# Three attention stages rewritten: dilated attention by query classes over 688 keys, values as split products over 512 queries

## The chip, the cores and the metric

One Trainium2 chip, one core of it. The number is the device time of one execution of the whole program in microseconds (us). A profiled execution gives, beside its own time, the span from its first to its last instruction and every instruction in it.

## What is computed

Two blocks over 1024 tokens of width 1024, everything in float32. The first block runs a differential attention and a neighbourhood attention (8 heads, each query sees 640 keys at most, with a bias table), an output product and a gate. The second block has two layers; each runs a dilated attention (8 heads of 64), a latent attention (8 heads, 96 wide in the scores, 64 in the values), an output product and an MLP. What the change touches are three of these attentions:

```python
DIL_CONFIGS = ((128, 1), (512, 4), (2048, 16))
def dilated_attention(q, k, v, pos, slopes):
    for window, dil in DIL_CONFIGS:      # query t attends to t + j*dil, |j*dil| <= window/2
        o, lse = dilated_branch(q, k, v, pos, slopes, window, dil)   # scores - slope[h]*|pos_q - pos_k|
    wts = jax.nn.softmax(jnp.stack(lses), axis=0)
    return jnp.sum(jnp.stack(outs) * wts[..., None], axis=0)
def latent_attention(...):
    s = (einsum(qn, k_nope) + einsum(qr, k_rot)) * scale
    p = softmax(s)                       # all 1024 keys
    return einsum(p, v)
```

The three branches of the dilated attention are one softmax in which a key counts once for every branch that holds it. Beyond a distance of 256 only keys at a multiple of 16 count, and from 64 to 256 only those at a multiple of 4.

## The kernel before

The program is written engine by engine, by hand: each engine (TensorE for products, ScalarE, VectorE, GpSimd, and SyncE, which issues most DMAs) runs its own list in the order in which it is written, and semaphores with counted values tie the lists together. Stages follow one another, with a barrier of all engines between them.

An attention stage has 64 units: 8 heads times 8 tiles of 128 queries. `softmax_pv_pe` gives TensorE's order: `scores(u+1)`, `turn(u)`, `pv(u-1)`. `scores` multiplies one 128-query tile by the keys into a pair of PSUM banks (512 columns each); keys and, in the latent stage, queries are held as two fp32r parts, a rounded high one and the rest, so that float32 precision comes out of two or three fp32r products. The maximum over the keys (`maxes`, VectorE) and the exponential (`exps`, ScalarE) follow. `turn` transposes the 128x128 tiles of the probabilities through TensorE; `copy_turned` brings them from PSUM to SBUF, half on ScalarE (L906), half on VectorE (L908). `pv` multiplies them by the values in plain float32, one product of 128 columns for each key tile (L881); the rows of this line count two instructions for each such product. `output` divides by the sum of the exponentials.

In the neighbourhood stage GpSimd makes the bias of each unit: once for each head it adds the column mask to a table `NAB` that SyncE has loaded (L1392, L1376), then for each unit it adds a row mask (L1395). In the dilated stage ScalarE scales a table of distances for each unit (L1427), GpSimd adds the logarithm of how often a key counts (L1400), over all 1024 keys.

After the latent stage `nt` transposes the attention's output for the output product: ScalarE writes the high part `XTh` (L492), VectorE the low one `XTl` (L529), both from PSUM.

## Time and profile before

| | |
|---|---|
| median of 3 executions | 4692.28 us (4685.75 to 4693.0) |
| the profiled execution | 4690.71 us, of which its span is 4688.9 us |
| neighbourhood attention | from 768 to 994 us in the span |
| dilated attention, two layers | from 1547 to 1815 and from 3274 to 3541 us |
| latent attention, two layers | from 1815 to about 2095 and from 3541 to about 3824 us |
| TensorE busy | 87% of the span |
| mean granted TensorE clock | 0.948 of 2.4 GHz |

The rows below are read so: a row of the timeline is start, duration, engine, line of the kernel, operation, output and inputs by the program's names, count; in brackets stands the idle time before it and what ended it. A matmul's duration is its latency; what it costs in a run of like ones is the distance from one start to the next. `PE` is TensorE, `DVE` VectorE, `ACT` ScalarE, `POOL` GpSimd, `SPq` SyncE's queue.

### The profile page before, as it was taken

The numbers are of one execution on the slowest core, as the hardware profiler recorded it, in microseconds if no ns is written. First come the engines' busy times: TensorE is split into PE (matmuls) and PEld (weight loads), VectorE is DVE, ScalarE is ACT, GpSimd is POOL, SyncE is SP. The second block draws the span as 40 slices with busy tenths as digits, with TensorE's granted clock in tenths as the row PEclk, the third lists the DMA queues.
The fourth block names the chain that finished last, engine by engine and source line by source line (L and its number), as shares of the span: only waits on it lengthen the run. The fifth ranks groups of instructions, "written<-read, shape, count | busy, mean of one in ns | idle before, by whom it ended". The sixth has DMA issues, their size and how long they took to land.

```text
span 4688.9 us, 60744 instructions
## 1 busy us (share of the span) xinstructions
PE 4082.2 (87%) x22152; PEld 3480.2 (74%) x22152; DVE 2228.0 (48%) x4269; ACT 1503.3 (32%) x2417; POOL 1736.7 (37%) x1140
## 2 busy tenths in 40 slices
PE   3999575788789798998899999688898996999998
PEld 2788465776577687886688888576887885888887
DVE  2443585532366565553444443465565544323323
ACT  2221243431233674441221211232773432222221
POOL 2432123531255462002544444353560003544442
PEclk9999888999899899998999999899999998999999
DMA  6765332631135422212223221245322221111111
GB/s 152 207 179 149 98 89 64 138 100 50 72 88 140 111 60 66 48 50 90 78 84 108 77 99 32 76 119 146 84 55 63 54 80 49 50 49 54 45 45 50
DMA packets 300704, 404.65 MB, mean 86 GB/s; under 512 B 45908, under 2 KB 224980, under 8 KB 299860
## 3 DMA queue, kind: packets, MB, share of 16 engines
q1 hardware_dynamic: 293496, 375.60, 28.5%
q10 hardware_dynamic: 6912, 25.17, 1.8%
q8 instruction: 178, 2.92, 0.3%
q14 instruction: 118, 0.97, 0.1%
HBM read 316.23 MB, written 93.63 MB: 87 GB/s over the span
## 4 chain that ended last, share of the span: by engine, by line
PE 68%; issue 8%; DVE 7%; POOL 5%; DMA 3%; SPq 2%; DVEq 2%; ACT 2%; POOLq 1%; ACTq 0%
PE ps L881 10%; PE ps L456 6%; PE ps L458 5%; PE ps L457 5%; PE ps L871 5%; PE ps L1834 5%; PE ps L1835 5%; PE ps L1836 5%; PE ps L1850 5%; PE ps L1852 4%; PE ps L1851 4%; POOL rs L770 2%; PE ps L917 1%; DVEq L1235 1%; PE ps L1507 1%
## 5 line engine op out<-in xcount | busy, mean ns | idle before, releaser
L405 POOL TENSOR_TENSOR WL<-RAW,WH 128x1024 fp32r<-128x1024 f32 x226 | 556.6, 2476 | 1195.1 <-ACT WH L387 1184.9
L456 PE MATMUL ps<-WH,XTh 128*128 128x512 f32 (+1 forms) x1536 | 616.9, 402 | 70.6 <-issue 34.8
L457 PE MATMUL ps<-WH,XTl 128*128 128x512 f32 (+1 forms) x1536 | 604.2, 393 | 0.0
L458 PE MATMUL ps<-WL,XTh 128*128 128x512 f32 (+1 forms) x1536 | 604.0, 393 | 0.0
L387 ACT ACTIVATE WH<-RAW 128x1024 fp32r<-128x1024 f32 x226 | 234.1, 1057 | 794.2 <-PE ps L1852 347.8
L1870 DVE TENSOR_TENSOR X<-ps,X 128x512 f32<-128x512 f32 x512 | 349.0, 689 | 254.1 <-PE ps L1852 253.1
L1850 PE MATMUL ps<-WH,Hh 128*128 128x512 f32 x1024 | 401.3, 392 | 4.3 <-DVE X L1870 4.0
L1834 PE MATMUL ps<-XTh,WH 128*128 128x512 f32 x1024 | 400.4, 391 | 1.2 <-issue 1.2
L1835 PE MATMUL ps<-XTl,WH 128*128 128x512 f32 x1024 | 398.9, 390 | 0.0
L1836 PE MATMUL ps<-XTh,WL 128*128 128x512 f32 x1024 | 398.8, 389 | 0.0
L1852 PE MATMUL ps<-WL,Hh 128*128 128x512 f32 x1024 | 398.6, 389 | 0.0
L1851 PE MATMUL ps<-WH,Hl 128*128 128x512 f32 x1024 | 398.5, 389 | 0.0
L456 PEld LDWEIGHTS ps<-WH,XTh 128*128 128x128 f32 x1536 | 296.5, 193 | 133.4 <-issue 72.0
L1400 POOL TENSOR_TENSOR BI<-BI,TB 128x1024 f32<-128x1024 f32 x128 | 303.5, 2373 | 225.7 <-ACT BI L1427 223.8
L1861 DVE TENSOR_TENSOR MT<-ps,MT 128x512 f32<-128x512 f32 x128 | 88.5, 692 | 609.1 <-ACT MT L1878 609.1
L458 PEld LDWEIGHTS ps<-WL,XTh 128*128 128x128 f32 x1536 | 295.3, 192 | 58.8
L457 PEld LDWEIGHTS ps<-WH,XTl 128*128 128x128 f32 x1536 | 296.6, 193 | 54.2
L1890 POOL TENSOR_TENSOR Hl<-MT,Hh 128x512 fp32r<-128x512 f32 x128 | 165.7, 1295 | 460.0 <-ACT Hh L1882 460.0
L881 PE MATMUL ps<-VS,PTr 128*128 128x128 f32 x2688 | 335.1, 277 | 0.0
L881 PEld LDWEIGHTS ps<-VS,PTr 128*128 128x128 f32 x2688 | 319.6, 194 | 0.0
L917 PE MATMUL ps<-KHs,QS 128*128 128x512 f32 (+1 forms) x512 | 218.4, 428 | 102.5 <-DMA slp<-slopes 40.8
L1411 DVE CUSTOM_DVE_ANT_0 Sb<-ps,BI 128x1024 f32<-128x1024 f32 (+1 forms) x192 | 209.5, 1091 | 171.6 <-PE ps L918 86.1
(196 smaller groups left out, 7664.0 us busy)
## 6 DMA issues: line engine op xcount, KB each, us to landing
RAW<-w_all SPq DMA_DIRECT2D x232, 512.0 KB, 4.0
WM<-w_mod ACTq DMA_DIRECT2D x48, 512.0 KB, 4.2
WM<-w_mod SPq DMA_DIRECT2D x48, 512.0 KB, 4.0
QS<-QA_d SPq DMA_DIRECT2D x24, 512.0 KB, 3.9
KHs<-KA_d SPq DMA_DIRECT2D x48, 256.0 KB, 6.0
KLs<-KA_d SPq DMA_DIRECT2D x48, 256.0 KB, 6.5
VS<-VA_d SPq DMA_DIRECT2D x20, 512.0 KB, 7.3
X<-x SPq DMA_DIRECT2D x2, 4096.0 KB, 12.8
```

The lines of the kernel that those rows point to most:

```text
L405: e.tensor_tensor(w_low(n), w_raw(n), w_high(n).bitcast(F32), ALU.subtract).then_inc(w_ready, 1)
L456: e.matmul(bank, a, w, start=(kc == 0), stop=False)
L457: e.matmul(bank, b, w, start=False, stop=False)
L458: j = e.matmul(bank, a, l, start=False, stop=(kc == K - 1))
L881: i = e.matmul(ps[:, 6 + u % 2, 0:P], ptbuf[:, u % 2, k, :], vbuf[:, h % 2, key, :], start=(k == 0), stop=(k == len(kt) - 1))
L1834: e.matmul(bank, w, xh, start=(kc == 0), stop=False)
L1835: e.matmul(bank, w, xl, start=False, stop=False)
L1836: j = e.matmul(bank, l, xh, start=False, stop=(kc == KC - 1))
L1850: e.matmul(bank, Hh[:, half, et, tq], w, start=(et == 0), stop=False)
L1851: e.matmul(bank, Hl[:, half, et, tq], w, start=False, stop=False)
L1852: j = e.matmul(bank, Hh[:, half, et, tq], l, start=False, stop=(et == 1))
L1870: e.tensor_tensor(X[:, t, cs], ps[:, 4 + (step * 16 + k) % (3 if mod else 4), :], X[:, t, cs], ALU.add).then_inc(s["yt"], 1)
```

## The change

The three stages get new code; the unit (128 queries of a head) and the number of units stay.

**Values in split parts over 512 queries.** In all three stages the transposed probabilities are now split like the keys: ScalarE writes the high part (`high`), VectorE the rest (`low`), into tiles `PTh` and `PTl` that hold a group of four units, 512 queries. The values are held side by side as high and low part, 64 columns each (`VHL`, made once for each head by `value_high` on ScalarE and `value_low` on GpSimd). `values` multiplies them with 512 query columns at a time as two fp32r products for each key tile. The result comes out transposed; `copy_out` brings it to SBUF, and four float32 products with `twoI` (two identity matrices, one above the other) turn it back and add the two halves. In the latent stage these stand in `turn_back` (L1723), in the other two ahead of the scores of every fourth unit (L1395), in columns of a score bank that the scores leave free.

**Dilated attention by classes.** A unit is now 128 queries of one class modulo four (every fourth query of one half of the sequence). Such a class needs 576 keys as they stand, and of the other 448 only those of its own class: 688 keys. Queries, and the far keys, are read with a stride of four elements. The bias is held in `ND` for all eight tiles of a head, scaled so that the next head's follows from it by adding a table to a quarter of the near and to all far columns (`dil_pool`); the queries' norm takes the head's slope up (`by_head`, one more small GpSimd instruction for each of 8 tiles in a layer).

**One more unit in flight.** In the neighbourhood and dilated stages (`band_pe`) there are three buffers of probabilities, scores run two units ahead, and the transposes are split: four tiles ahead of the scores, the rest behind the values.

Since the dilated output stands in class order, the `nt` behind the latent stage writes 4 of its 8 column blocks with a stride of four elements.

```diff
+DIL_FAR = 112
+DIL_KEYS = 576 + DIL_FAR
+N_UNITS, N_GROUPS = 64, 16
...
+                        to, got = XTh[:, kc, g * 512:g * 512 + 512], ps[:, turn_bank(n), :]
+                        if kc < classes:
+                            to, got = by_class(to), got.rearrange("p (r a) -> p r a", r=4)
+                        e.activation(to, got, ACT.Copy).then_inc(s["hi"], 1)
...
+        class Dilated:
...
+            def __init__(self, u):
+                g, c = divmod(u % T, 4)
+                self.g, self.first, self.width = g, 0, DIL_KEYS
...
+                self.queries = slice(512 * g + c, 512 * g + 512, 4)
+                if g == 0:
+                    far = slice(576 + c, S, 4)
...
+                    self.keys = [(slice(0, 512), 0), (slice(512, 576), 512), (far, 576)]
...
+        def band_pe(who, a):
...
+            def scores(u):
...
+                if u >= 2:
+                    e.wait_ge(s["max"], a.u0 + min(u - 1, N_UNITS))
+                if hosts_back(u - 2) is not None:
+                    e.wait_ge(s["out"], a.g0 + hosts_back(u - 2) + 1)
+                G = hosts_back(u)
+                if G is not None:
+                    e.wait_ge(s["ot_copied"], a.g0 + G + 1)
+                    for r in range(4):
+                        c = at.back + 64 * r
+                        j = e.matmul(flat(2 * (u % 2), c, c + 64), a.OT[:, G % 2, r * P:r * P + P], twoI[:], start=True, stop=True)
+                    j.then_inc(s["back"], 1)
...
+                for keys, c in at.keys:
+                    to = flat(2 * (u % 2), c, c + len(range(S)[keys]))
+                    e.matmul(to, Q[:, h % 2, at.queries], KH[:, h % 2, keys], start=True, stop=False)
+                    j = e.matmul(to, Q[:, h % 2, at.queries], KL[:, h % 2, keys], start=False, stop=True)
+                j.then_inc(s["full"], 1)
...
+            def turn_first(u):
+                at = band(a, u)
+                e.wait_ge(s["exp"], a.u0 + u + 1)
+                ge(e, s["lo"], 2 * (a.u0 + u) - 3)
+                for k in range(4):
+                    c = at.nat + k * P
+                    j = e.transpose(ps[:, 4 + u % 2, k * P:k * P + P], Pt[:, u % 3, c:c + P], ident[:])
+                j.then_inc(s["tr"], 1)
+            def turn_rest(u):
+                at = band(a, u)
+                ge(e, s["lo"], 2 * (a.u0 + u))
+                for src, c in at.rest:
+                    j = e.transpose(ps[0:src.stop - src.start, 7, c:c + P], Pt[:, u % 3, src], ident[:])
+                j.then_inc(s["tr"], 1)
...
+            def values(G, part):
...
+                    rows, key = (slice(0, 64), 4) if g == 0 else (slice(64, P), 3)
+                    v = a.VHL[rows, slot, key, :]
+                    e.matmul(ps[:, 6, :], v, a.PTh[rows, o, 4, :], start=False, stop=False)
+                    e.matmul(ps[:, 6, :], v, a.PTl[rows, o, 4, :], start=False, stop=False)
+                    for r in range(4):
+                        v, c = VFHL[:, slot, 4 * g + r, :], slice(r * P, r * P + P)
+                        e.matmul(ps[:, 6, c], v, a.PTh[0:DIL_FAR, o, 5, c], start=False, stop=False)
+                        j = e.matmul(ps[:, 6, c], v, a.PTl[0:DIL_FAR, o, 5, c], start=False, stop=(r == 3))
...
+            scores(0)
+            scores(1)
+            for u in range(N_UNITS + 6):
+                G, r = divmod(u - 1, 4)
+                if u < N_UNITS:
+                    turn_first(u)
+                scores(u + 2)
+                if 1 <= G <= N_GROUPS and r < 3:
+                    values(G - 1, r)
+                if u < N_UNITS:
+                    turn_rest(u)
...
+        def band_act(who, a):
...
+            def value_high(h):
+                e.wait_ge(*a.v_loaded(h // 2))
+                ge(e, s["ot"], a.g0 + 2 * h - 2)
+                o0 = 64 * (h % 2)
+                if a.kind == "dil":
+                    e.activation(VFHL[:, h % 2, :, 0:64], VFS[:, h // 2 % 2, :, o0:o0 + 64], ACT.Copy)
+                e.activation(a.VHL[:, h % 2, :, 0:64], a.VS[:, h // 2 % 2, :, o0:o0 + 64], ACT.Copy)
+                e.drain().then_inc(s["vhi"], 1)
+            value_high(0)
...
+            for u in range(N_UNITS + 6):
+                if 1 <= u <= N_UNITS:
+                    high(u - 1)
+                if u + 1 < N_UNITS:
+                    exps(u + 1)
+                if u % 4 == 0 and u >= 8:
+                    copy_out(u // 4 - 2)
+                if u % T == 5 and u + 3 < N_UNITS:
+                    value_high(u // T + 1)
...
+        def value_low(e, a, h):
...
+            e.tensor_tensor(a.VHL[:, h % 2, :, 64:128], a.VS[:, h // 2 % 2, :, o0:o0 + 64],
+                            a.VHL[:, h % 2, :, 0:64].bitcast(F32), ALU.subtract)
+            e.drain().then_inc(s["vlo"], 1)
...
+        def na_pool(who, a):
+            e, s = who.e, a.s
+            value_low(e, a, 0)
+            for u in range(N_UNITS):
+                h, t = divmod(u, T)
+                if t == 0:
+                    e.wait_ge(*a.loaded(h))
+                    nab = NAB[:, h % 2, :].rearrange("p (a b) -> p a b", b=GRID_W)
+                    e.tensor_tensor(nab, nab, rows3(CMK[:], NA_E, GRID_W), ALU.add)
+                    e.drain()
+                if u >= 3:
+                    e.wait_ge(s["max"], a.u0 + u - 2)
+                e0 = (NA_START[t] - 2 * t + 8) * GRID_W
+                e.tensor_tensor(BIn[:, u % 3, :], NAB[:, h % 2, e0:e0 + NA_KEYS], RMK[:, NA_KIND[t], :], ALU.add).then_inc(s["bias"], 1)
+                if u % T == 7 and u + 1 < N_UNITS:
+                    value_low(e, a, u // T + 1)
+        def dil_pool(who, a):
...
+                e.wait_ge(s["max"], a.u0 + u + 1)
+                if g == 0:
+                    parts = [(slice(c, 576, 4), slice(128, 272)), (slice(576, DIL_KEYS), slice(272, 384))]
+                else:
+                    parts = [(slice(0, DIL_FAR), slice(0, 112)), (slice(DIL_FAR + c, DIL_KEYS, 4), slice(112, 256))]
+                for cols, table in parts:
+                    j = e.tensor_tensor(ND[:, t, cols], ND[:, t, cols], LM[:, table], ALU.add)
+                j.then_inc(s["bias"], 1)
+                if t == 7:
+                    value_low(e, a, h + 1)
...
+        def heads_pe(who, a):
...
+            def values(G, part):
...
+                for n in range(3 * part, min(3 * part + 3, T)):
+                    v = a.VHL[:, h % 2, n, :]
+                    e.matmul(ps[:, 6, :], v, a.PTh[:, G % 2, n, :], start=(n == 0), stop=False)
+                    j = e.matmul(ps[:, 6, :], v, a.PTl[:, G % 2, n, :], start=False, stop=(n == T - 1))
+                if part == 2:
+                    j.then_inc(s["ot"], 1)
+            def turn_back(G):
+                e.wait_ge(s["ot_copied"], a.g0 + G + 1)
+                ge(e, s["out"], a.g0 + G)
+                for r in range(4):
+                    j = e.matmul(ps[:, 7, 64 * r:64 * r + 64], a.OT[:, G % 2, r * P:r * P + P], twoI[:], start=True, stop=True)
+                j.then_inc(s["back"], 1)
...
+            scores(0)
+            for u in range(N_UNITS + 4):
+                G, r = divmod(u, 4)
+                if u + 1 < N_UNITS:
+                    scores(u + 1)
+                if u < N_UNITS:
+                    turn(u)
+                if G >= 1 and r < 3:
+                    values(G - 1, r)
+                if G >= 1 and r == 3:
+                    turn_back(G - 1)
...
+        def heads_act(who, a):
...
+            def high(u):
+                G, r = divmod(u, 4)
+                if r == 0:
+                    ge(e, s["ot"], a.g0 + G - 1)
+                for b in range(2):
+                    e.wait_ge(s["tr"], 2 * (a.u0 + u) + 1 + b)
+                    e.activation(a.PTh[:, G % 2, 4 * b:4 * b + 4, r * P:r * P + P],
+                                 ps[:, 4 + b, :].rearrange("p (k q) -> p k q", q=P), ACT.Copy).then_inc(s["hi"], 1)
...
+        def heads_dve(who, a):
...
+            def low(u):
+                G, r = divmod(u, 4)
+                for b in range(2):
+                    e.wait_ge(s["hi"], 2 * (a.u0 + u) + 1 + b)
+                    at = (slice(None), G % 2, slice(4 * b, 4 * b + 4), slice(r * P, r * P + P))
+                    e.tensor_tensor(a.PTl[at], ps[:, 4 + b, :].rearrange("p (k q) -> p k q", q=P),
+                                    a.PTh[at].bitcast(F32), ALU.subtract).then_inc(s["lo"], 1)
```

TensorE's order in the latent stage before (`KMh`, `KMl` keys, `QMh`, `QMl` queries, `Pm` probabilities, `PTm` the same transposed, `VSm` values), one unit:

```order
L881 MATMUL ps<-VSm,PTm 128x128 x8
L1507 MATMUL ps<-KMh,QMh 128x512
L1508 MATMUL ps<-KMl,QMh 128x512
L1509 MATMUL ps<-KMh,QMl 128x512
L1507 MATMUL ps<-KMh,QMh 128x512
L1508 MATMUL ps<-KMl,QMh 128x512
L1509 MATMUL ps<-KMh,QMl 128x512
L871 MATMUL ps<-ident,Pm 128x128 x8
```

And now, from the last scores of a unit to the first of the next but one, at the fourth unit of one group and the first of the next:

```order
L1695 MATMUL ps<-KMh,QMl 128x512
L1703 MATMUL ps<-ident,Pm 128x128 x8
L1723 MATMUL ps<-twoI,OTm 128x64 x4
L1693 MATMUL ps<-KMh,QMh 128x512
...
L1703 MATMUL ps<-ident,Pm 128x128 x8
L1714 MATMUL ps<-PThm,VHLm 128x512
L1715 MATMUL ps<-PTlm,VHLm 128x512
L1714 MATMUL ps<-PThm,VHLm 128x512
L1715 MATMUL ps<-PTlm,VHLm 128x512
L1714 MATMUL ps<-PThm,VHLm 128x512
L1715 MATMUL ps<-PTlm,VHLm 128x512
```

The eight 128-column products behind every unit's transposes are gone; behind those of three units of four stand six, six and four 512-column ones, and behind the fourth the four that turn back.

TensorE's order in the dilated stage before (`QS` queries, `KHs`, `KLs` keys, `Pb` probabilities), one unit:

```order
L871 MATMUL ps<-ident,Pb 128x128 x8
L881 MATMUL ps<-VS,PTr 128x128 x8
L917 MATMUL ps<-KHs,QS 128x512
L918 MATMUL ps<-KLs,QS 128x512
L917 MATMUL ps<-KHs,QS 128x512
L918 MATMUL ps<-KLs,QS 128x512
```

And now (`Pd` probabilities, `VFHL` the values of the far keys), the iteration with the last third of a group's values:

```order
L1411 MATMUL ps<-ident,Pd 128x128 x4
L1401 MATMUL ps<-KHd,QSd 128x112
L1402 MATMUL ps<-KLd,QSd 128x112
L1401 MATMUL ps<-KHd,QSd 128x64
L1402 MATMUL ps<-KLd,QSd 128x64
L1401 MATMUL ps<-KHd,QSd 128x512
L1402 MATMUL ps<-KLd,QSd 128x512
L1441 MATMUL ps<-PThd,VHLd 128x512
L1442 MATMUL ps<-PTld,VHLd 128x512
L1445 MATMUL ps<-PThd,VFHL 128x128
L1446 MATMUL ps<-PTld,VFHL 128x128
...
L1418 MATMUL ps<-ident,Pd 112x128 x2
```

Two of the four 512-column score products are replaced by four narrow ones, and the transposes are six; L1445 and L1446 stand there four times each.

GpSimd's order in the neighbourhood stage before, at the change of a head, with what the instructions wait for (`heads_max` is VectorE's maximum, `na_ld` SyncE's loads of the head):

```order
L1395 TENSOR_TENSOR BI<-NAB,RMK 128x640 [waits heads_max] x7
L1392 TENSOR_TENSOR NAB<-NAB,CMK 128x1152 [waits heads_max,na_ld1]
L1395 TENSOR_TENSOR BI<-NAB,RMK 128x640
```

And now (`heads_vhi` is ScalarE's `value_high`, which stands behind the exponential of the head's seventh unit):

```order
L1597 TENSOR_TENSOR BIn<-NAB,RMK 128x640 [waits heads_max] x5
L1580 TENSOR_TENSOR VHLn<-VSn,VHLn 128x8x64 [waits heads_vhi]
L1592 TENSOR_TENSOR NAB<-NAB,CMK 128x1152 [waits na_ld1]
L1597 TENSOR_TENSOR BIn<-NAB,RMK 128x640 [waits heads_max] x8
```

The split of the next head's values has come between the last bias of a head and the table of the next, with a wait for ScalarE in front of it.

## Rows read from the trace of the kernel before

**Rows 1.** Windows by stage: us, busy time of each engine, granted clock, DMA share, GB/s

```profile
core 0: us, PE busy (x) PEld busy (x) DVE busy (x) ACT busy (x) POOL busy (x), PEclk, DMA share, GB/s
1547.00:1815.00 268.00, 240.44 (x1792) 214.52 (x1792) 159.65 (x387) 185.49 (x264) 151.75 (x64) 0.95 0.29 70
1815.00:2124.00 309.00, 286.89 (x2040) 260.60 (x2041) 167.53 (x336) 120.86 (x212) 9.39 (x4) 0.97 0.24 57
3274.00:3541.00 267.00, 240.49 (x1792) 214.79 (x1792) 159.63 (x387) 185.62 (x264) 151.77 (x64) 0.95 0.28 70
...
793.40:996.80 203.40, 160.84 (x1208) 150.21 (x1208) 108.06 (x384) 90.47 (x192) 115.13 (x70) 0.94 0.49 103
1566.00:1813.50 247.50, 236.84 (x1785) 212.04 (x1784) 158.67 (x384) 174.89 (x254) 150.64 (x64) 0.98 0.23 55
1825.40:2095.30 269.90, 264.42 (x1920) 241.59 (x1920) 158.06 (x320) 108.46 (x192) 0.00 (x0) 0.99 0.21 48
```

**Rows 2.** Timeline of TensorE, one unit of the latent stage

```profile
2019.38 0.48 PE L1507 MATMUL ps<-KMh,QMh 96*128 96x512 f32 x1
2019.70 0.40 PE L1508 MATMUL ps<-KMl,QMh 96*128 96x512 f32 x1
2019.94 0.39 PE L1509 MATMUL ps<-KMh,QMl 96*128 96x512 f32 x1
...
2020.85 1.04 PE L871 MATMUL ps<-ident,Pm 128*128 128x128 f32 x8
2021.73 1.95 PE L881 MATMUL ps<-VSm,PTm 128*128 128x128 f32 x16
2023.43 0.48 PE L1507 MATMUL ps<-KMh,QMh 96*128 96x512 f32 x1
```

**Rows 3.** Timeline of TensorE, one unit of the dilated stage

```profile
1607.10 1.06 PE L871 MATMUL ps<-ident,Pb 128*128 128x128 f32 x8
1608.00 1.95 PE L881 MATMUL ps<-VS,PTr 128*128 128x128 f32 x16
1609.70 0.48 PE L917 MATMUL ps<-KHs,QS 128*128 128x512 f32 x1
...
1610.72 1.04 PE L871 MATMUL ps<-ident,Pb 128*128 128x128 f32 x8
```

**Rows 4.** Timeline of TensorE: 320-column products in the neighbourhood stage

```profile
802.52 0.30 PE L918 MATMUL ps<-KLs,QS 128*128 128x320 f32 x1
802.67 0.31 PE L917 MATMUL ps<-KHs,QS 128*128 128x320 f32 x1
```

**Rows 5.** Timeline of TensorE: plain float32 products of one column

```profile
196.78 1.84 PE L1686 MATMUL ps<-ones,MA 128*128 128x1 f32 x16
198.49 0.48 PE L456 MATMUL ps<-WH,XTh 128*128 128x512 f32 x1
```

**Rows 6.** Groups by line and shape, latent stage

```profile
L1518 DVE TENSOR_REDUCE mx<-ps 128x1 f32<-128x1024 f32 x64 | 78.3, 1224 | 70.5 <-PE ps L1509 70.5
L1528 ACT ACTIVATE Pm<-ps,nmx 128x1024 f32<-128x1024 f32 x64 | 71.3, 1114 | 170.7 <-DVE nmx L1520 170.7
```

**Rows 7.** Timeline behind the latent stage: 512-column splits from PSUM

```profile
2096.13 4.03 ACT L492 ACTIVATE XTh<-ps 128x512 fp32r<-128x512 f32 x8 [4.51 <-PE ps L558]
2096.84 4.87 DVE L529 TENSOR_TENSOR XTl<-ps,XTh 128x512 fp32r<-128x512 f32 x8 [1.72 <-ACT XTh L492]
```

**Rows 8.** Groups by line and shape, neighbourhood stage

```profile
L1395 POOL TENSOR_TENSOR BI<-NAB,RMK 128x640 f32<-128x640 f32 x64 | 98.3, 1549 | 48.3 <-DVE nmx L1416 46.9
L1436 ACT ACTIVATE Pb<-Sb,nmx 128x640 f32<-128x640 f32 x64 | 53.1, 830 | 136.9 <-DVE nmx L1416 136.9
L1411 DVE CUSTOM_DVE_ANT_0 Sb<-ps,BI 128x640 f32<-128x640 f32 x64 | 52.8, 824 | 65.0 <-POOL BI L1395 53.1 <-PE ps L918 10.7 <-issue 0.4
L1392 POOL TENSOR_TENSOR NAB<-NAB,CMK 128x1152 f32<-128x1152 f32 x8 | 21.1, 2643 | 53.6 <-DMA NAB<-NAB_d 51.9 <-DVE nmx L1416 1.7
```

**Rows 9.** Groups by line and shape, whole span: smaller instructions of the new loops' kinds

```profile
L1890 POOL TENSOR_TENSOR Hl<-MT,Hh 128x512 fp32r<-128x512 f32 x128 | 165.7, 1295 | 460.0 <-ACT Hh L1882 460.0
L710 DVE TENSOR_TENSOR QN<-ps,rs 128x256 f32<-128x256 f32 x80 | 33.6, 420 | 66.9 <-POOL rs L770 65.5 <-PE ps L615 0.9 <-issue 0.4
L908 DVE COPY PTr<-ps 128x128 f32<-128x128 f32 x64 | 18.6, 291 | 8.5 <-PE ps L871 7.3 <-issue 0.3
L768 POOL TENSOR_TENSOR ss<-ss,epsr 128x8 f32<-128x8 f32 x32 | 6.4, 201 | 2.5 <-DVE ss L692 2.5
```

More of the change, by code:

```diff
@@ L110, in shape_tables, with times @@
     onehot[t5_bucket(rel), np.arange(2 * S - 1)] = 1.0
-    j = np.arange(TOEP)[None, :] - (T - 1) * P - np.arange(P)[:, None]
-    many = sum(((np.abs(j) <= w // 2) & (j % d == 0)).astype(np.int32) for w, d in DIL_CONFIGS)
-    logmult = np.where(many > 0, np.log(np.maximum(many, 1)), NEG).astype(np.float32)
+    def times(rel):
+        return sum(((np.abs(rel) <= w // 2) & (rel % d == 0)).astype(np.int32) for w, d in DIL_CONFIGS)
+    query = 4 * np.arange(P)[:, None]
+    many = times(np.arange(1536)[None] - 512 - query)
+    logmult = np.where(many > 0, 2 * np.log(np.maximum(many, 1)), -1e33).astype(np.float32)
+    many = times(4 * np.arange(-128, 256)[None] - query)
+    logstep = (2 * np.log(np.maximum(many, 1))).astype(np.float32)
     c = np.arange(GRID_W)
@@ L814, in in_cell, with qk_kind @@
             return lambda kc: (first + kc // kper, (kc % kper) * width)
-        def qk_kind(dst, gain, first):
+        def qk_kind(dst, gain, first, by_head=False):
             def store(e, t, m, slot):
@@ new lines, in build_program @@
+        class Narrow:
+            def __init__(self, u):
+                self.g = u % T // 4
+                t = u % T
+                self.first = na_tiles(t)[0] - 2 * self.g
+                self.flat, self.width, self.nat, self.back = 0, NA_KEYS, 0, 768
+                self.keys = [(slice(NA_START[t] * GRID_W, NA_START[t] * GRID_W + 512), 0),
+                             (slice(NA_START[t] * GRID_W + 512, NA_START[t] * GRID_W + NA_KEYS), 512)]
+                self.queries = tok(t)
+                self.rest = [(slice(512, NA_KEYS), 0)]
+                self.rest_rows = P
@@ L1976, in layout @@
     out["pos_cols"] = v["positions_2"][0].reshape(T, P).T
+    out["pos_class"] = v["positions_2"][0].reshape(2, P, 4).transpose(1, 0, 2).reshape(P, T)
     out["w_mod"] = v["w_mod_2"]
```

639 lines of the change are left out of this document (381 added, 258 removed).

## The prediction

> **What bounds the kernel now.** I read the windows by stage first, to see how much of the span the three rewritten stages hold: 203 us of the neighbourhood attention from its first maximum on, 268 and 267 us for the dilated in its two layers, and 270 us from the first scores of the latent stage to its last output [rows 1]. In the dilated and latent stretches TensorE is busy for 96% and 98% at a granted clock of 0.98 and more, VectorE and ScalarE for 71% or less. So these two are bound by TensorE, and its own timeline tells what a unit costs. The reader is to look at the distances of starts. Latent: scores to transposes 1.47 us (six 512-column fp32r products at 0.23, and about 0.1 for the change of kind), eight transposes 0.88, sixteen value instructions 1.70, that is 0.106 each; 4.05 in all [rows 2]. Dilated: 3.62, with scores of 1.02 [rows 3]. The neighbourhood stage is another matter: TensorE is busy for 161 of 203 us [rows 1], and GpSimd waits 52 us for the table of a head to land, while VectorE waits 53 us for GpSimd's bias [rows 8].
>
> **Prices on TensorE.** A 512-column fp32r product costs 0.227, a 320-column one 0.15 [rows 2, 4]: in proportion to columns. A plain float32 product is two instructions, and 16 of them take 1.71 us with one column as with 128, 0.107 each [rows 2, 5]; a transpose takes 0.11. I read 0.107 as the least that any product with a 128-column weight costs. Narrower fp32r products than 320 columns (64, 112, 128) are nowhere in the trace, nor operands with a stride of four elements. Lower bound 0.107 each, the floor; upper bound 0.213, the plain float32 product of two instructions [rows 2, 5]. I take 0.14, nearer to the 320-column row, which shows one pass for each column.
>
> The Trainium skill (SBUF — State Buffer, Door 1: The DMA port swizzle) states that SBUF has 16-byte lines and that an access which crosses to a new line each time pays, so float32 strides are free only inside one line. No row here has such a stride. The sum would be 0.107 by the floor and twice that for the strided loads by the rule; this speaks against the classes. Rival A has the same direction, with its price from rows.
>
> **Latent stage.** Removed: 1.70 of values in each unit. Added for four units: sixteen 512-column products, 3.63, with three changes of kind at 0.1, so 0.98 a unit; and four plain products, eight instructions at 0.107 with one change, 0.24 a unit. Unit: 1.47 + 0.88 + 0.98 + 0.24 = 3.57 against 4.05.
> Do the others keep up? ScalarE: exponential 1.11, two splits of 0.50 (8 in 4.03), a quarter of a copy 0.13: 2.3 [rows 6, 7]. VectorE: 1.22 for the maximum, which now negates itself, two low parts at 0.61, a quarter of an output 0.2: 2.65 [rows 6, 7]. The loop that could bind is transposes, two splits, next exponential, next transposes: the first half of the transposes with its latency 0.65, then 0.5 + 0.5 + 1.11 + 0.19 and hand-overs, about 3.0, under 3.57. So it is TensorE still. The stage holds 64 units: 270 - 64 x 4.05 = 11 of filling and emptying. The emptying grows, since three parts of values, a copy, the turning back and one output follow the last split: +3. New stretch 64 x 3.57 + 14 = 242, saves 28; two layers, **-56**. Bounds: 3.5 (smaller changes of kind) and 3.8 (the loop through ScalarE at a third longer), -65 and -27.
>
> **Dilated stage.** Scores: 0.454 for the two wide products, four narrow at 0.14, change 0.1: 1.11. Transposes: six at 0.11, 0.66. Values for four units: ten 512-column products 2.27, eight of 128 at 0.14 = 1.12, three changes: 0.92 a unit. Turning back 0.24. Sum 2.93; with all narrow ones at the floor 2.73, at 0.213 3.37. VectorE: maximum over 688, by the 640-column row 0.87 and the read behind it 0.1; low parts 0.61 and, for 256 columns, 0.42; output 0.2: 2.2 [rows 7 to 9]. ScalarE: 0.9 + 0.5 + 0.3 + 0.13 + 0.15 = 2.0 (the scaling of the distances is gone). GpSimd: the 640- and 1152-column rows give 0.2 + 0.00214 a column [rows 8], so two adds of 144 and 112 columns 0.95, and two value splits a head, 2 x 1.3 / 8 [rows 9]: 1.3, with eight units of slack. The third buffer lets scores run ahead, so that TensorE need not wait for a chain of 1.6 (split, exponential) inside 2.9.
> Start: the eight distance tiles, value splits and first biases come one after another; I put the second maximum where the first stood before, no gain. The stretch was 247.5 [rows 1], 64 x 3.62 = 232 and 15 around it; I leave 12, since the drains of TensorE at the end of each head go and the emptying is longer. 64 x 2.93 + 12 = 199.5, saves 48; two layers, **-96**. Bounds -122 and -40.
>
> **Neighbourhood stage.** TensorE: scores 0.454 + 2 x 0.14 + 0.1, five transposes 0.55, twelve value products a group (2.72 + 0.3) / 4, turning back 0.24: 2.4; VectorE 0.82 + 0.1 + 0.61 + 0.29 + 0.3 = 2.1 [rows 7 to 9]. The 52 us of waiting for the table should go: it is now asked for when the scores of the head before last are through, ahead of the values and gates, which come only once in two heads. Something is late next: at the change of a head GpSimd must wait for `value_high`, which stands behind the seventh exponential. From that unit's maximum: exponential 0.83, high part 0.5, low part 1.3, table 2.64, bias 1.55, hand-overs 0.5, 7.3 in all [rows 8, 9], where two units of 2.4 were to pass: 2.5 late, seven heads, 17. The first bias also waits for the values' load, now behind the table's, and their split: some 2.5 + 0.5 + 1.3, +4.5. New: 64 x 2.4 + 17 + 8 for emptying = 179 from the first maximum, against 203 [rows 1]; less 4.5: **-20**. Bounds: -45 (no lateness, 2.3 a unit), 0.
>
> **The rest.** The strided `nt` (8 of 16 evictions in a layer, at most doubled, 0.5 each) and the extra GpSimd instruction for 16 tiles (0.2 [rows 9], with a drain): +5, bounds 0 and +15.
>
> **Sum.** -56 - 96 - 20 + 5 = -167, on the profiled execution's 4690.7 us: 4524. The median of the runs shown lies 1.6 above it; I say **4523**.
>
> **Rivals.**
> *A. Narrow or strided products cost what plain float32 does.* For it: no row shows one cheap. Against: the 320-column row is in proportion to the 512-column one. Dilated units above 3.2, up to 3.37; neighbourhood 2.55. With 3.37: +0.44 x 128 + 0.15 x 64 = +66: 4589. Chance 0.25, from 4560 up. The rule of the Trainium skill cited above would come out here.
> *B. The floor everywhere, and no lateness at the heads.* -0.2 x 128 - 17 - 6, and some 8 in the latent stage: 4466. For it: three buffers may swallow the lateness. Chance 0.23, below 4490.
> *C. Slower: strided weights are read one by one.* All six products of a dilated unit load 128 queries with the stride. At a price p each the unit is 1.9 + 6p (1.9 is 2.93 without its six score products). It ends on the other side when the unit is 167 / 128 = 1.3 above 2.93, at p = 0.39, nearly four times the floor; at 0.5 the unit is 4.9, and the kernel 4523 + 252 = 4775. Nothing in the trace speaks for so much. Chance 0.04.
> *D. The gain goes back in waits.* The loop through ScalarE and VectorE locks both stages to about 4.0 and 3.5: 4690 or so. Against: the sums above leave 0.5 on the tightest. Chance 0.03.
>
> **Chances and range.** The forecast 0.45 (4490 to 4560), A 0.25, B 0.23, C 0.04, D 0.03. A difference of 0.2%, 9 us, is about what a measurement of this kernel can tell from none. Faster: the first three, 0.93; same 0.02 (part of D); slower 0.05 (C and a part of D). The range takes in most of A and B: 4445 to 4600.
>
> **What would show it.** Latent unit 3.57 between the starts of scores, TensorE without gaps, 16 value products at 0.227. In the dilated stage the distances of the 64-, 112- and 128-column products decide between forecast, A and C; 0.11 to 0.14 against 0.21 or more. VectorE or ScalarE busy over 90% of a stage would show my engine sums wrong. In the neighbourhood stage no wait for the load of `NAB`, and a wait of GpSimd in front of `VHLn` once a head, with VectorE's maximum late behind it by 2.5. Wrong I am if the narrow products cost more than two plain instructions, if a hand-over in the four-engine loop is longer than those seen, or if loads of strided far rows of the values are late.

## The result and the profile after

The changed kernel takes 4520.4 us (median of 4, 4515.2 to 4525.5) against 4689.0 (4684.7 to 4693.0): a ratio of 0.964, 95% interval 0.9624 to 0.9657. The forecast was 4523. That the total is right to 3 us owes something to chance: two terms of the sum were wrong by about 30 us each, in opposite directions. (The sum itself gives 4525, not 4523: 4690.7 - 167 is 4523.7, and the median stood 1.6 above the profiled execution, not under it.)

The profiled execution of the changed kernel took 4525.45 us, its span is 4523.6, its mean granted clock 0.942. To see the terms I cut both spans at TensorE's first score product of each stage and at the first transpose of the attention's output (`Y`) behind it. Three of these cuts in the changed kernel, and one of the kernel before, in TensorE's timeline:

```profile
1540.64 0.82 PE L1401 MATMUL ps<-KHd,QSd 128*128 128x512 f32 x1 [20.05 <-DMA KLd<-KA_d]
...
1772.15 0.76 PE L1693 MATMUL ps<-KMh,QMh 96*128 96x512 f32 x1 [11.15 <-DMA KMl<-KM_d]
...
2001.07 3.68 PE L580 MATMUL ps<-ident,Y 128*128 128x128 f32 x32 [1.06 <-DVEq L362]
```

```profile
1825.49 0.77 PE L1507 MATMUL ps<-KMh,QMh 96*128 96x512 f32 x1 [12.53 <-DMA VSm<-VM_d]
```

| from cut to cut, us | before | after | difference | forecast |
|---|---|---|---|---|
| neighbourhood | 208.0 | 187.5 | -20.5 | -20 |
| dilated, layer 1 and 2 | 263.1, 264.2 | 231.5, 233.9 | -61.9 | -96 |
| latent, layer 1 and 2 | 270.0, 271.6 | 228.9, 228.1 | -84.6 | -56 |
| all that lies between | 3412.1 | 3413.8 | +1.7 | +5 |
| span | 4688.9 | 4523.6 | -165.3 | -167 |

The windows of the changed kernel answer to [rows 1]: neighbourhood from its first maximum, dilated (layer 1) from its first maximum, latent in both layers. The window of the dilated stage before, 247.5 us, began 1.4 us ahead of its first maximum.

```profile
core 0: us, PE busy (x) PEld busy (x) DVE busy (x) ACT busy (x) POOL busy (x), PEclk, DMA share, GB/s
799.28:976.80 177.52, 148.27 (x889) 124.56 (x890) 133.40 (x304) 114.37 (x279) 123.59 (x77) 0.97 0.46 93
1542.70:1762.20 219.50, 210.85 (x1178) 191.17 (x1178) 131.63 (x288) 128.92 (x290) 91.75 (x148) 0.95 0.27 65
1772.10:2001.10 229.00, 224.19 (x1281) 190.56 (x1282) 163.42 (x224) 151.86 (x280) 10.25 (x8) 0.98 0.20 49
3428.80:3656.90 228.10, 222.30 (x1281) 188.87 (x1281) 163.33 (x224) 151.75 (x280) 10.24 (x8) 0.99 0.20 48
```

TensorE is still busy for 96% and more of the dilated and latent stretches, so it is still what bounds them, and the error must lie in the prices of its instructions. The neighbourhood stretch is 177.5 us long; the forecast said 179.

**A dilated unit**, answering to [rows 3]:

```profile
1644.05 0.38 PE L1418 MATMUL ps<-ident,Pd 128*128 128x128 f32 x2
1644.27 0.60 PE L1411 MATMUL ps<-ident,Pd 128*128 128x128 f32 x4
1644.63 0.60 PE L1401 MATMUL ps<-KHd,QSd 128*128 128x512 f32 x1
1645.06 0.40 PE L1402 MATMUL ps<-KLd,QSd 128*128 128x512 f32 x1
1645.30 0.19 PE L1401 MATMUL ps<-KHd,QSd 128*128 128x64 f32 x1
1645.33 0.40 PE L1402 MATMUL ps<-KLd,QSd 128*128 128x64 f32 x1
1645.56 0.45 PE L1401 MATMUL ps<-KHd,QSd 128*128 128x112 f32 x1
1645.83 0.41 PE L1402 MATMUL ps<-KLd,QSd 128*128 128x112 f32 x1
1646.07 0.44 PE L1436 MATMUL ps<-PThd,VHLd 128*128 128x512 f32 x1
...
1650.11 0.27 PE L1445 MATMUL ps<-PThd,VFHL 112*128 112x128 f32 x1
1650.21 0.28 PE L1446 MATMUL ps<-PTld,VFHL 112*128 112x128 f32 x1
```

Read the distances of starts. The six score products take 1.44 us (1644.63 to 1646.07) where I had 1.11, that is 0.24 each on average, as much as one of 512 columns. (Single distances between products of unequal width say little: here they run from 0.03 to 0.43, and the one of 0.43 is that of the first wide product in either order of the keys.) But the 128-column products of the far values (L1445, L1446), whose weights have no stride, cost 0.11. So the price is not one of narrow products. The weight loads (`PEld`) show where it sits; these are their groups in the dilated and then in the neighbourhood stage:

```profile
L1402 PEld LDWEIGHTS ps<-KLd,QSd 128*128 128x128 f32 x191 | 62.6, 328 | 0.4
L1401 PEld LDWEIGHTS ps<-KHd,QSd 128*128 128x128 f32 x190 | 60.9, 321 | 0.2
```

```profile
L1402 PEld LDWEIGHTS ps<-KLn,QSn 128*128 128x128 f32 x124 | 24.4, 196 | 2.8
L1401 PEld LDWEIGHTS ps<-KHn,QSn 128*128 128x128 f32 x124 | 24.1, 195 | 10.3 <-issue 7.5
```

The same 128x128 queries take 325 ns to load with the stride of four, 196 without, and in front of them the load path stands idle for 0.6 us in the whole stretch: they come back to back. Their own timeline, in the same unit:

```profile
1645.07 0.32 PEld L1401 LDWEIGHTS ps<-KHd,QSd 128*128 128x128 f32 x1
1645.30 0.31 PEld L1402 LDWEIGHTS ps<-KLd,QSd 128*128 128x128 f32 x1
```

One load starts 0.23 us after the other, and that is what each product costs.

**A latent unit**, answering to [rows 2]:

```profile
1885.87 1.04 PE L1703 MATMUL ps<-ident,Pm 128*128 128x128 f32 x8
1886.66 0.48 PE L1714 MATMUL ps<-PThm,VHLm 128*128 128x512 f32 x1
...
1888.14 0.40 PE L1693 MATMUL ps<-KMh,QMh 96*128 96x512 f32 x1
...
1889.53 1.04 PE L1703 MATMUL ps<-ident,Pm 128*128 128x128 f32 x8
```

Transposes 0.79 us, six value products 1.48 with the change of kind, six score products 1.39 without one. I had charged the change of 0.1 to both.

### The profile page after: what moved, and what is told of

It reads as the page before. It is cut to its first block, busy times and chain, and to the rows that moved or that the text cites. A ratio compares the mean times of both kernels' runs of the same rounds, so it can differ in the third digit from the quotient of the medians.

```text
span 4523.6 us, 53378 instructions
## 1 busy us (share of the span) xinstructions
PE 3936.4 (87%) x19336; PEld 3311.0 (73%) x19336; DVE 2218.5 (49%) x3805; ACT 1522.8 (34%) x2761; POOL 1658.0 (37%) x1369
## 4 chain that ended last, share of the span: by engine, by line
PE 68%; issue 8%; DVE 7%; POOL 5%; DVEq 3%; ACT 3%; DMA 2%; POOLq 2%; SPq 2%; ACTq 0%
PE ps L469 6%; PE ps L470 6%; PE ps L471 6%; PE ps L2181 5%; PE ps L2183 5%; PE ps L2182 5%; PE ps L2197 5%; PE ps L2199 5%; PE ps L2198 5%; PE ps L1703 2%; PE ps L1401 2%; PE ps L1402 2%; POOL rs L795 2%; PE ps L1411 1%; DVEq L1219 1%
## 5 line engine op out<-in xcount | busy, mean ns | idle before, releaser
L400 ACT ACTIVATE WH<-RAW 128x1024 fp32r<-128x1024 f32 x226 | 233.8, 1058 | 794.3 <-PE ps L2199 347.2
L2197 PEld LDWEIGHTS ps<-WH,Hh 128*128 128x128 f32 x1024 | 192.1, 188 | 52.9 <-DVE X L2217 13.6
L2225 ACT ACTIVATE MT<-ps 128x512 f32<-128x512 f32 x128 | 76.4, 597 | 452.6 <-PE ps L2183 449.1
L2181 PEld LDWEIGHTS ps<-XTh,WH 128*128 128x128 f32 x1024 | 192.6, 188 | 41.7 <-issue 2.0
L2183 PEld LDWEIGHTS ps<-XTh,WL 128*128 128x128 f32 x1024 | 192.5, 188 | 40.3
L2199 PEld LDWEIGHTS ps<-WL,Hh 128*128 128x128 f32 x1024 | 192.2, 188 | 40.3
```

The source lines that it names most:

```text
L400: e.activation(w_high(n), w_raw(n), ACT.Copy).then_inc(w_rounded, 1)
L2181: e.matmul(bank, w, xh, start=(kc == 0), stop=False)
L2183: j = e.matmul(bank, l, xh, start=False, stop=(kc == KC - 1))
L2197: e.matmul(bank, Hh[:, half, et, tq], w, start=(et == 0), stop=False)
L2199: j = e.matmul(bank, Hh[:, half, et, tq], l, start=False, stop=(et == 1))
```

## The experiments

Each is an edit of the changed kernel, which stands at 4520.4 us. The kernel before stood at 4687 to 4691 beside them. "In the stage" means from cut to cut as above.

**1. Queries as they stand.**

```diff
-                self.queries = slice(512 * g + c, 512 * g + 512, 4)
+                self.queries = tok(u % T)
```

> Left out: the classes on the query side. In the dilated stage the 128 queries of a unit are taken as they stand, without the stride of four; the far keys keep theirs, so the output is not that of the reference. All else as in the changed kernel. In the changed kernel a dilated unit takes 3.23 us on TensorE, of which the six score products with their change of kind hold 1.51. Theory S (the strided weights cost the time): two wide products 0.46, four narrow ones at 0.11 as in the neighbourhood stage, change 0.1, so 1.0; unit 2.72, 128 units: -65 us, about 4455; the weight loads of these products fall from 325 to about 190 ns. Rival M (the stride of the moving far keys, or narrowness itself, costs it): no change, 4520, and the loads may get shorter without effect.

Measured: 4457.3 (4453.6 to 4460.8), -63. The dilated stages take 199.5 and 202.4 us in place of 231.5 and 233.9. Eight groups of four units begin 86.7 us apart (1601.85 to 1688.59), 2.71 a unit. The loads as a group, two of them, and the six products of one unit, of the other half of the sequence; in the changed kernel such a unit's six take 1.59 (1657.30 to 1658.89):

```profile
L1402 PEld LDWEIGHTS ps<-KLd,QSd 128*128 128x128 f32 x186 | 36.5, 196 | 1.4
```

```profile
1643.69 0.19 PEld L1401 LDWEIGHTS ps<-KHd,QSd 128*128 128x128 f32 x1
1643.81 0.19 PEld L1402 LDWEIGHTS ps<-KLd,QSd 128*128 128x128 f32 x1
```

```profile
1643.50 0.34 PE L1401 MATMUL ps<-KHd,QSd 128*128 128x112 f32 x1
1643.65 0.30 PE L1402 MATMUL ps<-KLd,QSd 128*128 128x112 f32 x1
1643.76 0.24 PE L1401 MATMUL ps<-KHd,QSd 128*128 128x64 f32 x1
1643.83 0.28 PE L1402 MATMUL ps<-KLd,QSd 128*128 128x64 f32 x1
1643.95 0.48 PE L1401 MATMUL ps<-KHd,QSd 128*128 128x512 f32 x1
1644.26 0.39 PE L1402 MATMUL ps<-KLd,QSd 128*128 128x512 f32 x1
1644.49 0.38 PE L1418 MATMUL ps<-ident,Pd 128*128 128x128 f32 x2
```

0.99 us for the six, and the loads start 0.12 us apart. Theory S holds to 2 us.

**2. Far keys as they stand.**

```diff
-                    far = slice(576 + c, S, 4)
+                    far = slice(576 + DIL_FAR * c, 576 + DIL_FAR * c + DIL_FAR)
```

> Left out: the classes on the key side. In the dilated stage the 112 far keys of a unit are a contiguous block, the queries keep their stride of four; the output is not that of the reference. Theory S (strided weights): no change, 4520, the 112-column products keep distances of 0.23 to 0.27 us. Rival M (strided moving columns): the two 112-column products fall from about 0.25 to 0.11 each, -0.28 us a unit, 128 units: -36 us, about 4485.

Measured: 4518.4 (4515.9 to 4523.9), no change. A stride of four in the moving columns costs nothing that can be measured here, as long as the weights are what TensorE waits for. Experiment 1 says the same where the weights load quickly: its 112-column products still have the strided keys, and all four narrow ones take 0.45 us together. (The diff shows one half of the sequence; the other is changed alike.)

**3 and 4. Other strides.**

```diff
-                self.queries = slice(512 * g + c, 512 * g + 512, 4)
+                q0 = 512 * g + 256 * (c // 2) + c % 2
+                self.queries = slice(q0, q0 + 256 - c % 2, 2)
```

```diff
-                self.queries = slice(512 * g + c, 512 * g + 512, 4)
+                self.queries = slice(4 * g + c, S, 8)
```

> Changed: in the dilated stage the 128 queries of a unit are taken with a stride of two elements in place of four; the output is not that of the reference. Two of a unit's queries then stand in the same 16 bytes. If what counts is how many of a load's elements share 16 bytes and two are enough (the Trainium skill, SBUF - State Buffer, says so of reads), the loads take the unstrided time and the kernel is that of the run with contiguous queries, about 4455. If every stride costs alike, no change, 4520. If the cost grows with the bytes spanned, in between, about 4490, with loads of some 250 ns.

> Changed: in the dilated stage the 128 queries of a unit are taken with a stride of eight elements in place of four; the output is not that of the reference. If each element costs one access of 16 bytes wherever it stands, no change against the changed kernel: 4520, loads of 325 ns. If the cost grows with the stride, loads well over 400 ns, a unit above 3.8 us, and above 4590 in all.

Measured: stride two 4460.9 (4458.0 to 4469.8), as without a stride; stride eight 4535.1 in its one run. The loads, of stride two and then of eight:

```profile
L1402 PEld LDWEIGHTS ps<-KHd,QSd 128*128 128x128 f32 x183 | 36.5, 199 | 1.1
```

```profile
L1402 PEld LDWEIGHTS ps<-KLd,QSd 128*128 128x128 f32 x184 | 62.0, 337 | 0.2
```

196, 199, 325, 333 ns for strides of one, two, four, eight: a step between two and four, not a slope. The Trainium skill (SBUF — State Buffer, Door 1: The DMA port swizzle) says that two accesses to one 16-byte line are enough for full bandwidth, and float32 elements at a stride of two are just that. These runs agree, and the rule that the prediction set beside rival A came out in direction and, by the distance between loads (0.12 us without the stride, 0.23 with it), in size. Stride eight is 15 us above the changed kernel, of which some 7 stand in the dilated stages (236.9 and 236.0); with one run I make nothing of it.

**5. The value split later (neighbourhood).**

```diff
-                if u % T == 7 and u + 1 < N_UNITS:
-                    value_low(e, a, u // T + 1)
+                if t == 2 and h:
+                    value_low(e, a, h)
```

> Nothing is left out. In the neighbourhood stage GpSimd makes the low part of the next head's values behind the third bias of that head, not between the last bias of a head and the table of the next. In the changed kernel the half of a head with the change takes 12.1 us, the other 9.17, so 2.9 us are lost at each of 7 changes. Theory (GpSimd stands still for ScalarE's high part, 3.6 us, and then is late): the loss goes, 7 x 2.9 = -20, and the first bias comes 1.3 earlier: about 4499. Rival (GpSimd's own work of 16.4 us a head, or VectorE held up by it, sets the pace): at most half of it, 4510 to 4520.

Measured: 4504.8 (4499.0 to 4505.9), -15.6; in the stage 168.1 for 187.5, so -19.4. GpSimd at the change of a head in the changed kernel, and in this run:

```profile
858.08 1.29 POOL L1580 TENSOR_TENSOR VHLn<-VSn,VHLn 128x512 fp32r<-128x512 f32 x1 [3.61 <-ACTq L1499]
859.55 2.65 POOL L1592 TENSOR_TENSOR NAB<-NAB,CMK 128x1152 f32<-128x1152 f32 x1 [0.18 <-issue]
```

```profile
862.65 1.58 POOL L1597 TENSOR_TENSOR BIn<-NAB,RMK 128x640 f32<-128x640 f32 x1 [1.27 <-DVEq L1527]
864.19 2.65 POOL L1592 TENSOR_TENSOR NAB<-NAB,CMK 128x1152 f32<-128x1152 f32 x1
```

The wait of 3.61 us for ScalarE's high part is gone from in front of the table. VectorE's waits for a bias, other than the stage's first of 25 to 26 us, fall from 9.9 us to 0.7. The half of a head with the change goes from 12.1 to 10.05 us, the other from 9.17 to 8.88, so a difference of 1.2 stays between them. The first bias did not come earlier, as I had expected (8.4 us behind the first scores, 8.3 in the changed kernel): the first head's split still stands in front of its table.

**6. Queries copied by class.** The diff is cut: `queries` is `tok(u % T)` as in experiment 1, and TensorE reads `QCd` and waits for `qc`.

```diff
+            def by_classes(h):
+                e.wait_ge(*a.loaded(h))
+                e.activation(QCd[:, h % 2, :].rearrange("p (g r i) -> p g r i", g=2, r=4),
+                             QSd[:, h % 2, :].bitcast(F32).rearrange("p (g i r) -> p g r i", g=2, r=4), ACT.Copy).then_inc(s["qc"], 1)
...
+                if a.kind == "dil" and u % T == 3 and u + 5 < N_UNITS:
+                    by_classes(u // T + 1)
```

> Nothing is left out. In the dilated stage ScalarE copies each head's queries once into the order of the classes (a strided read of 1024 columns, one instruction a head, at the fourth unit of the head before), and TensorE loads them from there without a stride. Theory S: the gain of the run with contiguous queries, 63 us, less what the copy costs: ahead of the first scores some 1.5 us in each layer, and ScalarE goes from 2.35 to about 2.55 us a unit, still under 2.72: about 4462. Rival: ScalarE becomes the bound or the exponential behind the copy is late once a head (2 x 8 x 1.5 = 24): about 4485.

Measured: 4470.1 (4466.7 to 4478.0), -50; in the stages 202.5 and 204.5. That lies between theory (4462) and rival (4485), nearer to the theory. The copy takes longer than I reckoned from a contiguous one of 1024 columns:

```profile
L1506 ACT ACTIVATE QCd<-QSd 128x1024 fp32r<-128x1024 f32 x7 | 14.5, 2067 | 0.0
```

**7. Scores one unit ahead.**

```diff
-            scores(1)
-            for u in range(N_UNITS + 6):
+            for u in range(N_UNITS + 7):
                 G, r = divmod(u - 1, 4)
+                scores(u + 1)
                 if u < N_UNITS:
                     turn_first(u)
-                scores(u + 2)
```

> Nothing is left out. In the neighbourhood and dilated stages the scores run one unit ahead, not two: they stand ahead of the first transposes of the unit before, as in the kernel before. Theory (the dilated stage is TensorE's alone, and one unit of lead covers maximum and exponential, 2.2 us, with 2.9 us of other work of TensorE): nothing in the dilated stage; in the neighbourhood stage 2.3 us stand against 2.2, so 0 to 0.2 a unit: 4520 to 4533. Rival (the third buffer is what lets TensorE run without gaps): 0.3 us a unit in all three stretches, 192 units, +58: 4578.

Measured: 4734.8 (4733.0 to 4741.2), slower by 214 than the changed kernel, and by 43 than the kernel before beside it. Both theories miss. In the stages: neighbourhood 243.1 for 187.5, dilated 306.6 and 310.5. Two of the waits of the dilated stage, from 1620 to 1780 us (engine, line, what it waited for; us in all, times, longest):

```profile
DVE Pd L1524 <- PE ps L1402: 82.8, 36, 4.0
...
PEld ps L1418 <- DVE PTld L1540: 30.6, 27, 1.9
```

The last transposes of a unit wait for the low parts of the unit before; on VectorE these stand behind the next maximum, which waits for scores that TensorE has only just made. I had counted the cover of the exponential, and not this ring.

**8. One ahead, low parts first.** The same, with VectorE's order turned:

```diff
-                if u + 1 < N_UNITS:
-                    maxes(u + 1)
                 if 1 <= u <= N_UNITS:
                     low(u - 1)
+                if u + 1 < N_UNITS:
+                    maxes(u + 1)
```

> Nothing is left out. As the run with the scores one unit ahead, but VectorE makes the low parts of a unit ahead of the maximum of the unit after the next, not behind it. Theory (what cost 214 us there was a ring: the last transposes of a unit wait for the low parts of the unit before, these stand on VectorE behind a maximum, and that waits for scores which TensorE has only just done): the ring is open, the dilated stage back at 3.23 us a unit, the neighbourhood stage at 2.3 to 2.5, 4520 to 4535. Rival (the second unit of lead is needed as such, for maximum and exponential): waits for the exponential take the place of those for the low parts, 4700 or more.

Measured: 4642.8 (4639.3 to 4649.5), +122. The order of VectorE was 92 of the 214 us; the other 122 stay as long as the scores run only one unit ahead. Dilated 257.8 and 260.6, neighbourhood 244.3. The chain in the dilated stage, VectorE and then ScalarE:

```profile
1680.32 0.86 DVE L1524 CUSTOM_DVE_ANT_0 Pd<-ps,ND 128x688 f32<-128x688 f32 x1
...
1682.73 0.69 DVE L1536 TENSOR_TENSOR PTld<-ps,PThd 128x512 fp32r<-128x512 f32 x1 [1.54 <-ACT PThd L1479]
...
1683.67 0.86 DVE L1524 CUSTOM_DVE_ANT_0 Pd<-ps,ND 128x688 f32<-128x688 f32 x1
```

```profile
1681.25 0.87 ACT L1468 ACTIVATE Pd<-Pd,mx 128x688 f32<-128x688 f32 x1 [1.63 <-DVEq L1526]
...
1682.12 0.58 ACT L1479 ACTIVATE PThd<-ps 128x512 fp32r<-128x512 f32 x1
```

Maximum, exponential, high part, low part and the next maximum now follow one after another, 3.35 us from maximum to maximum: two engines take turns. One or two maxima in a group of four come later (3.84 or 4.61 us), so that eight units take 29.05 us (1634.02 to 1663.07), 3.63 each; that is 0.40 over the changed kernel's 3.23, and 64 x 0.40 is the 26 us by which the stage is longer. It is neither of the two theories as I wrote them: the waits are between ScalarE and VectorE, and TensorE waits little for the exponential (2.3 us from 1620 to 1780, where VectorE waits 73 us for ScalarE's high part and ScalarE 72 for the maximum).

**9. Latent values in one block.**

```diff
-                if G >= 1 and r < 3:
-                    values(G - 1, r)
+                if G >= 1 and r == 0:
+                    for part in range(3):
+                        values(G - 1, part)
```

> Nothing is left out. In the latent stage all sixteen value products of a group stand behind the first unit's transposes of the next group, in place of six, six and four behind three units. If a change from a plain float32 or transposing product to an fp32r one costs 0.1 us and a change between values and scores nothing, a group has one such change for each unit in both kernels (five with the turning back), and TensorE's group stays at 13.65 us: 4520, or a little over it where the next exponential is late behind the long block. If each visit of the values costs a change of its own, two visits fewer: 0.2 a group, 32 groups, -6: 4514.

Measured: 4568.9 in one run, +48; the latent stages 248.9 and 247.6 for 228.9 and 228.1. A group takes 14.95 us. Two of its four units now hold only scores and transposes, and there TensorE waits for the exponential:

```profile
1907.28 0.39 PE L1695 MATMUL ps<-KMh,QMl 96*128 96x512 f32 x1
1908.11 1.09 PE L1703 MATMUL ps<-ident,Pm 128*128 128x128 f32 x8 [0.45 <-ACT Pm L1745]
...
1911.04 1.09 PE L1703 MATMUL ps<-ident,Pm 128*128 128x128 f32 x8 [0.45 <-ACT Pm L1745]
```

2.93 us from one to the next: that is the loop through ScalarE, for which the forecast had about 3.0. From the last product's 0.23 us (1907.51) to 1908.11 TensorE does nothing for 0.6 us, twice a group, 1.2 of the 1.3 us that a group is longer; nothing is left for a change of kind that was saved. Both forecasts miss: the late exponential that the first allowed for costs 48 us, not a little.

**10. The turned output as it stands.**

```diff
-                turned = nt(who, TURN, 2 + L, Y, False, out0, classes=4)
+                turned = nt(who, TURN, 2 + L, Y, False, out0)
```

> Changed: the transposed attention output of the second block is written as it stands, not with the stride of four, in all eight column blocks; the columns of the dilated half are then in class order and the output is not the reference's. The first eight evictions took 5.80 us on ScalarE and 6.41 on VectorE in the changed kernel against 4.03 and 4.87, and the first product came 0.6 us later behind the first transposes. Theory (TensorE waits for the last eviction only at the start of the product): 0.6 to 1.5 us a layer, -1 to -3: 4518. Rival (every strided eviction counts, 16 a layer on two engines by 0.25 to 0.4): -8 to -10: 4511.

Measured: 4522.1 (4514.3 to 4528.0), no change. The evictions are as short as before again (611 ns on ScalarE, 743 with the stride) and the time doesn't follow, so the rival's 8 to 10 us aren't there; the theory's 1 to 3 us can't be told from none.

**11. Both repairs.** The edits of 5 and 6; the first head's copy stands behind the second distance tile.

> Nothing is left out. Two repairs together: the queries of the dilated stage copied by class on ScalarE (the first head's copy now stands behind the second distance tile, and has its own load to wait for), and GpSimd's split of the next values behind the third bias in the neighbourhood stage. Their single runs gave -50 and -16 us; the first scores of a dilated stage waited some 5 us longer in the former, because the copy stood behind all sixteen distance instructions, and most of that, 2 x 4, should come back: 4520 - 50 - 16 - 8 = 4446. If the two share a cause they would give less, 4455 to 4470; they stand in different stages with a barrier between, so I expect the sum.

Measured: 4454.9 (4449.1 to 4457.3), 0.9496 of the kernel before (0.9482 to 0.951). It is 65.5 us under the changed kernel, the sum of the single gains (15.6 and 50.3) and no more: moving the first copy brought nothing. The first scores do come some 3 us earlier than in experiment 6 (563.4 and 1194.8 us after the transposes of `Y`, 566.2 and 1198.4 there; the changed kernel has 563.9 and 1193.9). But in the first layer the stage itself lasts 207.9 us in place of 202.5; in the second it is 204.9 and 204.5. The trace shows most of it for the first layer: the first exponential stands 6.6 us behind the first scores (2.9 in experiment 6), since twelve distance instructions and a wait of 2.47 us for the load of the far values are ahead of it on ScalarE. Counted from the transposes of `Y` it comes at 570.0 us, against 569.1: what was moved was not the last thing to be waited for. No run tests this.

## Why the prediction was right, and where not

**What bounds it.** Right: TensorE bounds the dilated and latent stages before and after, at the distances of starts. In the changed kernel VectorE is busy for 60% to 72% of these stretches, ScalarE for 59% to 67%.

**Latent, -56 against -84.6; outside the bounds I gave.** The mechanism was right, the size was not. A group of four units takes 13.65 us, 3.41 a unit, where the sum had 3.57. By its parts, of a group: turning back 0.81 us a group (forecast 0.96), scores 5.63 (5.88), transposes 3.24 (3.52), values 3.97 (3.93). The step at fault is "1.47 + 0.88": both were read where each unit had a change of kind in front of its scores and plain products behind its transposes. Now three of four scores follow the values, which are of their kind (1.39 each), and three of four transposes are followed by fp32r products (0.79). Filling and emptying is 228.9 - 64 x 3.41 = 10.6 us, not 14: the +3 for a longer emptying was wrong too, and is 7 of the 28.6 us by which the forecast missed. Experiment 9 shows that the number of visits to the values is not what counts.

**Dilated, -96 against -61.9.** The step "four narrow at 0.14" failed, in both halves. Narrow products as such cost the floor, 0.11 (L1445 here, and the four narrow scores in experiment 1 on average). With weights at a stride of four, every product costs about 0.235 however few its columns are, for a load starts only every 0.23 us: 6 x 0.235 and the change of 0.1 are the 1.51 us that the scores take in a unit, +0.40 on my sum; transposes are less by 0.05, and values and turning back by 0.04 each: 3.23 measured (12.77 and 13.05 us for alternate groups of four; the parts are those of the shorter), 2.93 forecast. By the prediction's own sign, a dilated unit above 3.2, rival A came out in this stage, and the total of 4520 hides it: the latent stage gave back 28.6 of the 34 us. It is rival A's mechanism for the stride only; at 3.37 it charged the narrow value products too. Rival C named the cause most closely, a price for each strided weight load, but set it at 0.39 and more where 0.235 was measured. Experiments 1 to 4 settle it: unstrided weights give 2.71 a unit (the prediction's sum with all narrow products at the floor was 2.73) and take back 63 us, unstrided moving columns nothing. The emptying, 219.5 - 64 x 3.23 = 12.8, was right.

**Neighbourhood, -20 against -20.5.** The mechanism was right; that the size is right to 0.5 us is partly luck, since the parts err both ways. The halves of a head without a change take 9.17 us (2.29 a unit, forecast 2.4), those with one 12.1, so 2.9 late at a change, forecast 2.5. The emptying is 177.5 - 64 x 2.29 - 7 x 2.9 = 10.6 us, forecast 8. The first maximum is 5.9 us later in the span than before (799.28, 793.39), forecast 4.5. GpSimd does wait for ScalarE ahead of `VHLn`, and the waits of 52 us for the table are gone [rows 8]. Experiment 5 takes VectorE's wait for the late bias away; the stage is 19.4 us shorter.

**The rest, +5 against +1.7.** The strided evictions of `nt` are longer (743 ns on ScalarE over all, 615 before) and cost nothing that experiment 10 could measure.

**The third buffer and the second unit of lead.** I gave them a sentence, and no term: "TensorE need not wait for a chain of 1.6 inside 2.9". The sign was right; experiments 7 and 8 show how much hangs on it. With the other engines' orders as they are, one unit of lead costs 214 us, more than the whole change gains; with VectorE's turned, still 122. In the neighbourhood stage some of that goes with the clock: granted 0.86 in experiment 8, with TensorE busy for 179 of 236 us, against 0.97 and 148 of 177.5 in the changed kernel, for the same products.

## What to carry to other kernels

Price a product by its weight load as well as its columns: a narrow one is cheap only if its weights load quickly, and float32 weights at a stride of four elements do not; one strided copy of them on an engine with room pays at once. Where engines pass a unit round, write down for each wait what stands ahead of it on the engine waited for; the lead in units is a property of all the orders together, and can be worth more than the arithmetic saved.

## What the runs showed of the hardware

- Weight loads of 128x128 fp32r: 196 ns contiguous, 199 at stride two, 325 at four, 333 at eight. In a run of such loads a product costs about 0.11 us at least with the first two and 0.24 with the others. ScalarE pays for the stride as well: 2.07 us for the copy of 1024 columns at a stride of four, where a contiguous split of that width (L400) takes 1.06 on average; whether the stride itself or the pattern of eight blocks costs the rest, no run separates.
- VectorE stood still behind GpSimd. The gate product (L1560) reads two operands from SBUF. It takes 0.42 or 0.43 us in four of its sixteen instructions, three of them at the end of the stage, with GpSimd idle; six take 0.73 to 0.75, beside the end of a bias, and six 2.01 to 2.04, when GpSimd is at its table:

```profile
859.96 0.43 DVE L1558 TENSOR_TENSOR TMPn<-ps,li 128x256 f32<-128x256 f32 x1
860.47 2.01 DVE L1560 TENSOR_TENSOR Y<-TMPn,ZSn 128x256 f32<-128x256 f32 x1
...
966.65 0.43 DVE L1560 TENSOR_TENSOR Y<-TMPn,ZSn 128x256 f32<-128x256 f32 x1
```

GpSimd's L1592 runs from 859.55 to 862.20 (rows of experiment 5), and VectorE's instruction ends 0.28 us after it. The product just ahead, which reads PSUM, isn't held up. The Trainium skill (SBUF — State Buffer, SBUF: two separate sides) says that VectorE with two SBUF inputs and GpSimd, where it reads SBUF as here, exclude each other for a whole instruction; this row agrees, save that the instruction ends only 0.28 us behind GpSimd's where it takes 0.43 when undisturbed.
